# A mixture-of-experts decoder layer on one core: token rows of an expert pair picked by a 0/1 product from SBUF instead of gathered from memory

## The chip, the core and the metric

The kernel is one program on one NeuronCore of a Trainium2 chip. Its engines are PE (TensorE, matrix products), DVE (VectorE), ACT (ScalarE), POOL (GpSimd) and SP (SyncE, which here only issues transfers). The metric is the device time of one execution in microseconds, as the median of several runs: 1571.71 us for the kernel before (1568.71 to 1578.26 in 3 runs).

## The reference

One decoder layer in float32, width 2048, on 256 prompt tokens and 8 sample tokens, each of these with a cache of 2048 past positions in pages of 128. What matters here is the last part, the experts:

```python
lg = uf @ w_rg + b_rg                       # 4 groups, top-1
le = einsum('td,gde->tge', uf, w_re) + b_re # 8 experts in the group, top-2
comb = sum(one_hot(eid, 32) * gate[..., None], axis=1)
h = silu(einsum('td,edf->tef', u, w_gate)) * einsum('td,edf->tef', u, w_up)
h = h * comb[:, :, None]
return einsum('tef,efd->td', h, w_down)     # 32 experts, 2048 -> 256 -> 2048
```

The kernel computes each expert only for the tokens that chose it. Each of the 256 prompt tokens chooses two experts, so 512 rows of 2048 floats (8 KB) go to experts.

## The kernel before

**Stages.** The first part, `attention_and_route`, runs over 128 steps (`STEPS`), one page of a sample's cache in each. SP loads key and value pages into rings; DVE scores the keys, PE multiplies the values (`values`, L967). Between the pages the steps carry the prompt's projection, its attention heads, the output projection and, from step `ROUTE` = 111, the router. Step 122 (`PLACE`) has DVE build one-hot tables that say which token sits in which slot of which expert block; `slots` on PE (step 125) turns them into index lists by small matmuls.

**Token rows.** In steps 115 to 122 PE transposes the normalised tokens (`token_rows`, L1110), ACT copies them to the tile `qo` (L1336), 128 tokens at a time, and stores them as rows in the memory buffer `u_rows` (L1340). After the last page, POOL gathers by the index list `idx` the rows of the first two experts into `xg` (L952), a DMA with an index for each partition. PE turns them with 16 transposes (`first_tokens`, L1155) and ACT copies the result to `xgT` (L1346). Then come the sample tokens' own output projection (L1171) and sums, and a barrier.

**Expert pairs.** The second part, `experts`, works on two experts at a time, 16 pairs; each expert has 64 slots. For a pair SP loads six blocks of 2 MB (gate, up and down weights of two experts) into six slots of the tile `ws`, each as soon as PE has used the block that lay in it: `gu0`, `gu1` free gate and up, `y0`, `y1` free down. All go through one queue, in the order gate, up, gate, up, down, down. PE does for a pair n: gate and up of the first expert (L1931, L1933), of the second, then transposes of the first result (`turn_over`, L1940), the token rows of pair n+1 (`tokens`, 16 transposes, L1921), `turn_over` of the second, and the down products of both (L1953). Before these it waits until ACT has copied the next `xgT` (L2030). POOL gathers the rows of pair n+2 (L1853) once PE has transposed those of n+1, as there is one `xg`, and then scatters pair n's results to `y_rows` (L1867). A flag `many2` chooses between gathers of 64 and 128 indices; indices without a token are skipped. Up to five extra pairs for crowded experts stand behind flags, and none is used in these runs. In the first pair PE, DVE and ACT also do the sample tokens' routing (L1960, L1968, L2063), and ACT turns to the pair only after it.

At the end SP reads `y_rows` back, DVE adds and normalises, and the output is stored.

Of the kernel before, what the change touches and what calls it, by code (L numbers as in the profile page):

```python
# [50 lines left out]
C_SEMS = ("gsq gss gms gsqrt on od h sq2 ss2 ms2 sqrt2 un lp lpc lgp rt rcopy rst iota ex mask cnt pe2 oh idxp idx "  # L51
# [129 lines left out]
def hybrid_step(nc, a, outs, u_rows, y_rows):  # L181
    (y_prompt, y_sample, sbk_p, sbv_p, fxk_p, fxv_p, logf_p, sbk_s, sbv_s, fxk_s, fxv_s, logf_s) = outs
    ctx = ExitStack()
    with ctx:
# [28 lines left out]
        xg = sb("xg", [P, D])  # L213
        xgT = sb("xgT", [P, KC, P])
        idx = sb("idx", [P, PAIRS], I32)
# [4 lines left out]
        many2 = sb("many2", [1, PAIRS], I32)  # L220
# [72 lines left out]
        class start:  # L293
# [296 lines left out]
            def vector(dve):  # L590
# [90 lines left out]
                for i in range(PAGES, 2 * PAGES):  # L681
                    score_half(i)
                    if i == PAGES:
# [5 lines left out]
                            cTs, FB, ptr, ws, W, kring, vring, qb, Z, key_caches, value_caches, w_in, bank, S, C, E, wr, br, xg, xgT, idx, dest,  # L689
                            gates, extra, many, many2, iota, destc, drow, xs_pc, g_pc, sqs, srs, outs, u_rows, start, A,  # L690
# [5 lines left out]
        experts(nc, ctx, ws, W, a, ident, ones, iota, gcol, lastq, xT, xn, xgT, xg, wr, br, bank, sem, E, idx, dest, gates, extra,  # L696
                many, many2, destc, drow, sqs, srs, y_prompt, y_sample, u_rows, y_rows)
# [19 lines left out]
HALF = SLOTS // 2  # L717

# [63 lines left out]
def attention_and_route(nc, a, ident, ones, tri_ge, tri_lt, neg_sb, neg_fx, pick, lastq, seg, gcol, xT, xn, qo, lf, qpart,  # L782
                        cTs, FB, ptr, ws, W, kring, vring, qb, Z, key_caches, value_caches, w_in, bank, S, C, E, wr, br, xg, xgT, idx, dest,
                        gates, extra, many, many2, iota, destc, drow, xs_pc, g_pc, sqs, srs, outs, u_rows, start, A,
# [7 lines left out]
    with ctx:  # L792
# [21 lines left out]
        ohs = take(2, 2, P)  # L814
        ohb = take(2, 2, PAIRS)
        ohb2 = take(2, 2, BLOCKS)
# [3 lines left out]
        slot_of = take(P)  # L820
# [5 lines left out]
        tok, tokc = take(3), take(3)  # L826
# [4 lines left out]
        ohs2 = rstd.rearrange("p t s -> p (t s)").rearrange("p (t k s) -> p t k s", t=2, k=2)  # L831
# [78 lines left out]
        def _(pool):  # L910
# [14 lines left out]
            own.step(pool.tensor_scalar(tokc[:, :], tok[:, :], -1.0, float(T), ALU.mult, ALU.add))  # L925
            own.step(pool.memset(manyf[:, :], 1.0))
            own.step(pool.iota(io32[:, :].rearrange("p (h b s) -> p h b s", h=2, b=2), [[HALF, 2], [SLOTS, 2], [1, HALF]],
                               base=0, channel_multiplier=0))
            own.step(pool.tensor_copy(slot_of[:, :], io32[:, :]))
# [16 lines left out]
            pool.wait_ge(S["bcast"], NB)  # L946
            own.step(pool.memset(xg[:, :], 0.0))
            pool.wait_ge(C["idx"], 1)
            pool.wait_ge(C["rst"], 32)
            for n in range(2):  # L950
                wait_past(pool, E["xgp"], 4 * n)
                pool.indirect_dma_start(xg[:, :], None, u_rows[0:SEQ, :],  # L952
                                        bass.IndirectOffsetOnAxis(ap=idx[:, n:n + 1], axis=0),
                                        bounds_check=SEQ - 1, oob_is_err=False).then_inc(E["xg"], 16)

        @block.tensor
        def _(pe):
# [177 lines left out]
            def slots():  # L1135
                pe.wait_ge(C["oh"], 1)
                pe.wait_ge(S["done2"], 1)
                for i in range(4):
                    pe.matmul(bank[7][:, 0:PAIRS], ohs[:, i // 2, i % 2, :], ohb[:, i // 2, i % 2, :],
                              start=(i == 0), stop=(i == 3))  # L1140
                pe.wait_ge(C["oh"], 2)
                for i in range(4):
                    mm = pe.matmul(bank[7][:, PAIRS:PAIRS + BLOCKS], ohs2[:, i // 2, i % 2, :], ohb2[:, i // 2, i % 2, :],
                                   start=(i == 0), stop=(i == 3))
                mm.then_inc(C["idxp"], 1)

            def first_tokens():
                pe.wait_ge(E["xg"], 16)
# [1079 lines left out]
```

## Time and profile before

| | |
|---|---|
| median of 3 runs | 1571.71 us (1568.71 to 1578.26) |
| profiled execution | 1566.98 us, span 1565.2 us |
| mean granted TensorE clock | 0.903 |
| busy: PE / DVE / ACT / POOL | 81% / 43% / 15% / 4% |
| read from memory, written | 568.74 MB, 17.77 MB |
| queue 0 (POOL's indirect transfers) | 4432 packets, 9.05 MB, 1.8% |
| stages | steps with pages to about 948 us, experts from 999 us, last weights landed about 1516 us |

The span runs from the first to the last instruction of the profiled execution. A granted clock of 1.00 is 2.4 GHz and 0.50 is 1.2 GHz. The DMA share is the mean busy share of the core's 16 DMA engines. PE's matmuls in float32 appear as two records each, its transposes as one.

### The profile page before, as it was taken

What the parts mean: (1) busy time and instruction counts of PE and PEld (TensorE: products, weight loads), DVE (VectorE), ACT (ScalarE), POOL (GpSimd) and SP (SyncE); (2) the same over time, 40 slices, a digit from 0 to 9 for tenths busy, and PEclk for the clock granted to TensorE, in tenths of its full rate; (3) what the DMA queues carried; (4) which work ended last, traced back from release to release, by engine and by line L of the source; (5) the groups of instructions that cost most, each with busy time, mean ns of one, the idle gap of its engine ahead of it and who ended that gap; (6) DMA issues with size and microseconds to landing.
All of it is one profiled execution on the core that took longest, in us unless ns stands there. A gap on an engine that the chain in (4) does not pass through costs nothing. (4 is left out here: it accounts for less than half of the span.)

```text
span 1565.2 us, 24701 instructions
## 1 busy us (share of the span) xinstructions
PE 1274.4 (81%) x7862; PEld 806.4 (52%) x7863; DVE 672.5 (43%) x4782; ACT 229.8 (15%) x453; POOL 61.8 (4%) x107
## 2 busy tenths in 40 slices
PE   7999788889889798847999977788787778678783
PEld 5777455556556466424667533544444444344451
DVE  4536855757657576758664671121000001000004
ACT  2121002212122122111020111011000010100011
POOL 1000000000000000001000000001000000100000
PEclk9999999999899899867999996789899998888996
DMA  9767999999999999999999899989999999999974
GB/s 310 269 205 292 389 389 394 384 392 375 375 400 378 382 396 372 410 402 374 374 403 402 330 410 367 422 346 415 399 421 382 390 389 371 369 387 386 376 338 172
DMA packets 173996, 576.64 MB, mean 368 GB/s; under 512 B 18457, under 2 KB 78666, under 8 KB 160058
## 3 DMA queue, kind: packets, MB, share of 16 engines
q1 hardware_dynamic: 145616, 541.70, 89.6%
q10 hardware_dynamic: 23842, 24.68, 4.6%
q0 software_dynamic: 4432, 9.05, 1.8%
q8 instruction: 42, 0.69, 0.2%
q14 instruction: 64, 0.52, 0.1%
HBM read 568.74 MB, written 17.77 MB: 375 GB/s over the span
## 5 line engine op out<-in xcount | busy, mean ns | idle before, releaser
L128 DVE CUSTOM_DVE_ANT_0 ws<-ws,xgT 128x128 f32<-128x128 f32 x1792 | 388.1, 284 | 200.9 <-DMA ws<-in_cache_fox_k 173.0
L1931 PE MATMUL bank<-ws,xgT 128*64 128x256 f32 x1024 | 261.0, 420 | 103.7 <-DMA ws<-in_w_expert_up 99.4
L982 PE MATMUL bank<-xn,ws 128*128 128x264 f32 x1152 | 291.0, 408 | 7.9 <-DMA ws<-in_w_in 7.9
L982 PEld LDWEIGHTS bank<-xn,ws 128*128 128x128 f32 x1152 | 223.8, 200 | 109.3 <-issue 55.5
L1933 PE MATMUL bank<-ws,xgT 128*64 128x256 f32 x1024 | 261.1, 420 | 0.0
L1931 PEld LDWEIGHTS bank<-ws,xgT 128*64 128x64 f32 x1024 | 152.9, 152 | 209.4 <-DMA ws<-in_w_expert_up 110.2
L967 PE MATMUL bank<-ws,PR 128*32 128x512 f32 x1024 | 149.2, 663 | 80.5 <-DMA ws<-in_cache_fox_v 76.2
L2131 DVE COPY gu<-bank 128x256 f32<-128x256 f32 x32 | 13.6, 425 | 386.9 <-PE bank L1933 386.9
L1933 PEld LDWEIGHTS bank<-ws,xgT 128*64 128x64 f32 x1024 | 152.8, 152 | 0.0
L128 DVE DVE_READ_ACCUMULATOR2_ANT Z<- 128x1 f32 x1792 | 142.1, 79 | 0.0
L1953 PE MATMUL bank<-ws,hT 128*32 128x512 f32 x1024 | 116.1, 606 | 12.3 <-ACT xgT L2030 12.1
L1087 PE MATMUL bank<-qo,ws 128*128 128x256 f32 x512 | 118.5, 391 | 5.6 <-DVE qo L1532 4.6
L1087 PEld LDWEIGHTS bank<-qo,ws 128*128 128x128 f32 x512 | 98.8, 195 | 31.1 <-issue 14.8
L521 PE MATMUL bank<-xn,ws 128*128 128x264 f32 x384 | 86.8, 387 | 0.0
L967 PEld LDWEIGHTS bank<-ws,PR 128*32 128x32 f32 x1024 | 21.5, 112 | 121.2 <-DMA ws<-in_cache_fox_v 90.3
L521 PEld LDWEIGHTS bank<-xn,ws 128*128 128x128 f32 x384 | 72.6, 190 | 14.1 <-issue 2.0
L1953 PEld LDWEIGHTS bank<-ws,hT 128*32 128x32 f32 x1024 | 32.4, 112 | 84.5 <-issue 69.6
L605 DVE CUSTOM_DVE_ANT_0 ws<-ws,xgT 128x128 f32<-128x128 f32 x256 | 55.3, 286 | 39.2 <-DMA ws<-in_cache_sb_k 14.6
L2038 ACT ACTIVATE si<-bank 128x128 f32<-128x128 f32 x32 | 8.8, 276 | 323.0 <-PE bank L1940 323.0
L2142 DVE COPY ys<-bank 128x512 f32<-128x512 f32 x32 | 20.6, 686 | 56.7 <-PE bank L1953 56.7
L1256 ACT ACTIVATE blk<-bank 128x264 f32<-128x264 f32 (+1 forms) x40 | 16.4, 410 | 180.5 <-PE bank L982 122.3
L1867 POOL DMA_INDIRECT y_rows<-ys,dest x32 | 29.1, 910 | 161.5 <-DVE ys L2142 124.5
(439 smaller groups left out, 979.0 us busy)
## 6 DMA issues: line engine op xcount, KB each, us to landing
ws<-in_cache_sb_k SPq DMA_DIRECT2D x128, 512.0 KB, 8.3
ws<-in_cache_fox_k SPq DMA_DIRECT2D x128, 512.0 KB, 12.9
ws<-in_cache_sb_v SPq DMA_DIRECT2D x128, 512.0 KB, 8.9
ws<-in_cache_fox_v SPq DMA_DIRECT2D x128, 512.0 KB, 12.7
ws<-in_w_expert_gate SPq DMA_DIRECT2D x32, 2048.0 KB, 21.9
ws<-in_w_expert_up SPq DMA_DIRECT2D x32, 2048.0 KB, 26.4
ws<-in_w_expert_down SPq DMA_DIRECT2D x32, 2048.0 KB, 25.4
ws<-in_w_in SPq DMA_DIRECT2D x24, 2048.0 KB, 21.3
```

The lines of the kernel that those rows point to most:

```text
L128: ins = dve.tensor_tensor_reduce(k, k, qb[:, (g * H + h) * HD:(g * H + h + 1) * HD], 1.0, 0.0, ALU.mult, ALU.add, Z[:, n % 2, g, h, t:t + 1])
L521: mm = pe.matmul(bank[4 + k % 4][:, 0:T], chunk(n)[:, c, m * P:(m + 1) * P], xn[:, c, :], start=(c == 0), stop=(c == KC - 1))
L605: ins = dve.tensor_tensor_reduce(k, k, qb[:, (g * H + h) * HD:(g * H + h + 1) * HD], 1.0, 0.0, ALU.mult, ALU.add, Z[:, 0, g, h, t:t + 1])
L967: mm = pe.matmul(bank[0][r0:r0 + 32, :], PR[:, g, t, :], vring[:, u, g, half * 512:(half + 1) * 512], start=(t == 0), stop=(t == PAGES - 1))
L982: mm = pe.matmul(out[:, 0:T], w[:, c, m * P:(m + 1) * P], xn[:, c, :], start=(c == 0), stop=(c == KC - 1))
L1087: mm = pe.matmul(out, ws[:, 4 + r, k0:k0 + P], qo[:, 8 * r + c, 0:SEQ], start=(r == 0 and c == 0 and m % 2 == 0), stop=(r == 1 and c == 7) ...
L1256: nc.scalar.activation(out, src, ACT.Copy).then_inc(S[done], 1)
L1867: pool.indirect_dma_start(y_half, bass.IndirectOffsetOnAxis(ap=dest[0:rows, 2 * n + k:2 * n + k + 1], axis=0), ys[k][0:rows, :], None, bou ...
L1931: pe.matmul(bank[2 * k][0:SLOTS, 0:256], lhs, ws[:, wg, c * 256:(c + 1) * 256], start=(c == 0), stop=(c == KC - 1))
L1933: mm = pe.matmul(bank[2 * k][SLOTS:P, 0:256], lhs, ws[:, wu, c * 256:(c + 1) * 256], start=(c == 0), stop=(c == KC - 1))
L1953: mm = pe.matmul(bank[4 + 2 * k + dc][q * HALF:(q + 1) * HALF, :], hT[k][:, j, h0:h0 + HALF], ws[:, wd, d0:d0 + 512], start=(j == 0), stop ...
L2142: dve.tensor_copy(ys[0][:, i * 512:(i + 1) * 512], bank[4 + i][:, :]).then_inc(E["yc0"], 1)
```

## The change

The tokens stay in `qo`. ACT now writes them so that `token_cols(qo, t, c)` is a block of 128 tokens by 128 of the 2048 columns, side by side; the store to `u_rows` and the gathers are gone. DVE's tables are kept: `in_slot` (is this the token's slot within the pair) and `in_pair` (is this its pair), in the room of `xg`. For each pair POOL multiplies them and adds the two choices of a token: `pick_tok[:, i, t, :]`, 128 tokens by 128 slots of zeros and ones, in two buffers. PE multiplies: for each of 16 column blocks two matmuls of 128x128 (one for each half of the tokens), which add up to the block of `xgT` that the transposes gave. PE's loop over pairs is written out for two pairs a turn, because of the two buffers, and the extra pairs are written out without a loop. `slots` loses the matmuls for `idx`, DVE its steps for `idx` and `many2`; `place` on DVE additionally waits for the last broadcast of queries, which has used the same tile.

PE, end of the first part, before. The names are: `ws<-...PR` value pages, `blk` the tables, `osum` and `pick` the last sample's output.

```order
L967 MATMUL bank<-ws,PR 32x512 x12
L1139 MATMUL bank<-blk 128x21 x4
L1143 MATMUL bank<-blk 128x42 x4
L967 MATMUL bank<-ws,PR 32x512 x8
L1055 MATMUL bank<-pick,osum 128x4 x4
L1155 MATMUL bank<-ident,xg 128x2x2x32 x16
L1161 MATMUL bank<-sred,ones 128x16
L1171 MATMUL bank<-ws,qo 32x512 x64
```

The same place in the changed kernel:

```order
L964 MATMUL bank<-ws,PR 32x512 x12
L1136 MATMUL bank<-blk 128x42 x4
L964 MATMUL bank<-ws,PR 32x512 x8
L1052 MATMUL bank<-pick,osum 128x4 x4
L1148 MATMUL bank<-xg,qo 128x128 x32
L1155 MATMUL bank<-sred,ones 128x16
L1165 MATMUL bank<-ws,qo 32x512 x64
```

Four matmuls of `slots` are gone, and 32 matmuls stand where 16 transposes stood.

PE in the loop over pairs, from the last gate and up matmul to the down products, before (`gu` the gate and up results, `hT` the input of down):

```order
L1933 MATMUL bank<-ws,xgT 64x256
L1940 MATMUL bank<-ident,gu 128x128 x2
L1914 ISA
L79 REGISTER_ALU
L1921 MATMUL bank<-ident,xg 128x2x2x32 x16
L1940 MATMUL bank<-ident,gu 128x128 x2
L1997 REGISTER_ALU
L1953 MATMUL bank<-ws,hT 32x512 x32
```

And in the changed kernel:

```order
L1914 MATMUL bank<-ws,xgT 64x256
L1919 REGISTER_ALU
L1921 MATMUL bank<-ident,gu 128x128 x2
L79 REGISTER_ALU
L1901 MATMUL bank<-xg,qo 128x128 x32
L1921 MATMUL bank<-ident,gu 128x128 x2
L1978 REGISTER_ALU
L1934 MATMUL bank<-ws,hT 32x512 x32
```

The place is the same, the rows' operands come from `qo` and the table, and there are 32 matmuls for 16 transposes.

The diff, cut to its core:

```diff
+        in_slot = xg[:, 0:4 * P].rearrange("p (t k s) -> p t k s", t=2, k=2)
+        in_pair = xg[:, 512:512 + 4 * PAIRS].rearrange("p (t k n) -> p t k n", t=2, k=2)
+        pick_tmp = xg[:, 640:640 + 4 * P].rearrange("p (t k s) -> p t k s", t=2, k=2)
+        pick_tok = xg[:, 1152:1152 + 4 * P].rearrange("p (i t s) -> p i t s", i=2, t=2)
...
+def token_cols(qo, t, c):
+
+    return qo[:, 8 * t + c // 2, c % 2 * P:(c % 2 + 1) * P]
...
-            pool.wait_ge(S["bcast"], NB)
-            own.step(pool.memset(xg[:, :], 0.0))
-            pool.wait_ge(C["idx"], 1)
-            pool.wait_ge(C["rst"], 32)
+            pool.wait_ge(C["oh"], 1)
             for n in range(2):
-                wait_past(pool, E["xgp"], 4 * n)
-                pool.indirect_dma_start(xg[:, :], None, u_rows[0:SEQ, :],
-                                        bass.IndirectOffsetOnAxis(ap=idx[:, n:n + 1], axis=0),
-                                        bounds_check=SEQ - 1, oob_is_err=False).then_inc(E["xg"], 16)
+                own.step(pool.tensor_tensor(pick_tmp.rearrange("p t k s -> p (t k) s"), in_slot.rearrange("p t k s -> p (t k) s"),
+                                            over(in_pair[:, :, :, n].rearrange("p t k -> p (t k)"), P), ALU.mult))
+                pool.tensor_tensor(pick_tok[:, n, :, :], pick_tmp[:, :, 0, :], pick_tmp[:, :, 1, :], ALU.add).then_inc(E["xg"], 1)
+                pool.wait_ge(E["xg"], n + 1)
...
             def first_tokens():
-                pe.wait_ge(E["xg"], 16)
+                pe.wait_ge(E["xg"], 1)
...
                 for k in range(4):
                     for c in range(4):
-                        out = bank[4 + k][:, c * P:(c + 1) * P].rearrange("p (b h s) -> p h b s", b=2, h=2)
-                        mm = pe.transpose(out, xv[:, 4 * k + c, :], ident[:, :])
+                        for t in range(2):
+                            mm = pe.matmul(bank[4 + k][:, c * P:(c + 1) * P], token_cols(qo, t, 4 * k + c), pick_tok[:, 0, t, :],
+                                           start=(t == 0), stop=(t == 1))
                     mm.then_inc(E["xgp"], 1)
...
             def token_rows(i):
                 t, k = divmod(i, 4)
                 act.wait_ge(C["rt"], i + 1)
-                h0 = 8 * t + 2 * k
-                nc.scalar.activation(qo[:, h0:h0 + 2, 0:SEQ], bank[(4, 6)[i % 2]][:, :].rearrange("p (a f) -> p a f", a=2),
+                to = qo[:, 8 * t:8 * t + 8, 0:SEQ].rearrange("p a (b f) -> p a b f", b=2)[:, :, :, 32 * k:32 * k + 32]
+                nc.scalar.activation(to, bank[(4, 6)[i % 2]][:, :].rearrange("p (f a b) -> p a b f", a=8, b=2),
                                      ACT.Copy).then_inc(C["rcopy"], 1)
-                if k == 3:
-                    act.wait_ge(C["rcopy"], i + 1)
-                    act.dma_start(u_rows[t * P:(t + 1) * P, :].rearrange("p (a f) -> p a f", f=SEQ),
-                                  qo[:, 8 * t:8 * t + 8, 0:SEQ]).then_inc(C["rst"], 16)
...
             def tokens(n):
 
-                rest = pool.value_load(many2[0:1, n:n + 1], min_val=0, max_val=1)
-                wait_past(pool, E["xgp"], 4 * n)
-                with pool.If(rest > 0):
-                    gather(n, P)
-                with pool.Else():
-                    gather(n, SLOTS)
+                pool.tensor_tensor(pick_tmp.rearrange("p t k s -> p (t k) s"), in_slot.rearrange("p t k s -> p (t k) s"),
+                                   over(in_pair[:, :, :, n].rearrange("p t k -> p (t k)"), P), ALU.mult).then_inc(E["sel"], 1)
+                pool.wait_ge(E["sel"], n - 1)
+                wait_past(pool, E["xgp"], 4 * n - 4)
+                pool.tensor_tensor(pick_tok[:, n % 2, :, :], pick_tmp[:, :, 0, :], pick_tmp[:, :, 1, :], ALU.add).then_inc(E["xg"], 1)
+                pool.wait_ge(E["xg"], n + 1)
...
-            with pe.Fori(1, EXP_PAIRS - 1) as n:
-                pair(n, True)
+            with pe.Fori(0, EXP_PAIRS // 2 - 1) as m:
+                for i in range(2):
+                    pair(2 * m + 1 + i, True, i=i)
```

## Rows read from the trace of the kernel before

**Rows 1.** The page: DMA queues (packets, MB, share), chain of waits.

```profile
q10 hardware_dynamic: 23842, 24.68, 4.6%
q0 software_dynamic: 4432, 9.05, 1.8%
DMA ws<-in_w_expert_up 23%; PE bank L1931 8%; PE bank L1953 1%; DMA ws<-y_rows 1%; SPq L170 0%; PE bank L1933 0%; PE bank L1960 0%; DVE ws L2173 0%; DMA y_rows<-ys,dest 0%; DVE ws L2162 0%; DVE ws L2156 0%; ACT xgT L2030 0%; ACT L2038 0%; DVEq L1813 0%; PE bank L1968 0%
```

**Rows 2.** Windows: us, busy time by engine, granted clock, DMA share, GB/s.

```profile
915.00:948.00 33.00, 23.75 (x146) 10.03 (x138) 19.48 (x80) 3.68 (x7) 0.38 (x1) 0.79 1.04 408
1050.00:1500.00 450.00, 351.09 (x2862) 193.09 (x2862) 36.93 (x83) 46.98 (x110) 36.34 (x39) 0.90 0.99 391
964.00:969.00 5.00, 5.00 (x32) 1.28 (x28) 0.00 (x0) 0.00 (x0) 0.00 (x0) 0.58 0.62 199
1033.00:1038.00 5.00, 5.00 (x36) 1.29 (x32) 0.83 (x2) 0.00 (x0) 0.00 (x0) 0.65 0.15 31
```

**Rows 3.** Timeline of SP: start, us, what; second gate load of two pairs.

```profile
1149.28 0.33 SPq L170 DMA_DIRECT2D ws<-in_w_expert_gate  x1
...
1492.84 0.33 SPq L170 DMA_DIRECT2D ws<-in_w_expert_gate  x1
```

**Rows 4.** Timeline of one steady pair's turn, with the idle time before in brackets.

```profile
1252.98 0.51 PE L1940 MATMUL bank<-ident,gu 128*128 128x128 f32 x2
...
1253.32 1.97 PE L1921 MATMUL bank<-ident,xg 128*128 128x128 f32 x16
...
1255.93 7.07 PE L1953 MATMUL bank<-ws,hT 128*32 128x512 f32 x64 [0.40 <-ACT xgT L2030]
...
1269.07 0.69 PE L1931 MATMUL bank<-ws,xgT 128*64 128x256 f32 x1 [6.07 <-DMA ws<-in_w_expert_up]
...
1277.83 0.33 SPq L170 DMA_DIRECT2D ws<-in_w_expert_gate  x1
...
1279.79 0.43 PE L1931 MATMUL bank<-ws,xgT 128*64 128x256 f32 x1 [2.16 <-DMA ws<-in_w_expert_up]
```

**Rows 5.** Timeline of the end of the first part.

```profile
934.01 0.69 DVE L1600 TENSOR_TENSOR blk<-blk 128x512 f32<-128x512 f32 x1
...
939.25 1.93 PE L967 MATMUL bank<-ws,PR 128*32 128x512 f32 x8 [1.29 <-DMA ws<-in_cache_fox_v]
...
948.83 1.05 PE L1055 MATMUL bank<-pick,osum 128*128 128x4 f32 x8 [0.73 <-issue]
...
956.35 3.68 PE L1155 MATMUL bank<-ident,xg 128*128 128x128 f32 x16 [6.46 <-DMA xg<-u_rows,idx]
```

**Rows 6.** Timeline and groups of PE (busy, mean ns): float32 matmuls of 128x128.

```profile
44.28 1.05 PE L538 MATMUL bank<-zx,blk 128*128 128x128 f32 x8
...
L538 PE MATMUL bank<-zx,blk 128*128 128x128 f32 x16 | 2.1, 275 | 0.0
```

**Rows 7.** Windows of 1 us, columns as in rows 2.

```profile
948.00:949.00 1.00, 0.27 (x6) 0.17 (x2) 0.00 (x0) 0.60 (x1) 0.76 (x1) 1.00 1.05 391
1255.00:1256.00 1.00, 0.60 (x9) 0.41 (x11) 0.00 (x0) 1.00 (x3) 0.00 (x0) 1.00 0.80 295
1269.00:1270.00 1.00, 0.93 (x6) 0.55 (x8) 0.00 (x0) 0.00 (x0) 0.00 (x0) 0.50 1.11 463
```

**Rows 8.** Timeline of PE and of ACT in the first pair.

```profile
1030.49 10.03 PE L1953 MATMUL bank<-ws,hT 128*32 128x512 f32 x64 [6.59 <-ACT xgT L2030]
...
1028.59 1.85 ACT L2030 ACTIVATE xgT<-bank 128x448 f32<-128x448 f32 x4
```

**Rows 9.** Timeline of POOL: a cast, a steady pair's gather.

```profile
711.11 0.33 POOL L922 CAST iota<-io 128x128 f32<-128x128 int32 x1
...
1220.60 0.96 POOL L1853 DMA_INDIRECT xg<-u_rows,idx  x1 [24.80 <-PE bank L1921]
```

**Rows 10.** Windows of 6 us in two turns, columns as in rows 2.

```profile
1156.00:1162.00 6.00, 3.05 (x32) 0.65 (x20) 1.07 (x2) 1.08 (x2) 1.77 (x2) 1.00 1.01 423
1225.00:1231.00 6.00, 2.36 (x24) 0.52 (x16) 0.37 (x1) 1.09 (x2) 1.99 (x2) 1.00 1.02 262
```

More of the change, by code:

```diff
@@ L695, in hybrid_step @@
         bctx.close()
-        experts(nc, ctx, ws, W, a, ident, ones, iota, gcol, lastq, xT, xn, xgT, xg, wr, br, bank, sem, E, idx, dest, gates, extra,
-                many, many2, destc, drow, sqs, srs, y_prompt, y_sample, u_rows, y_rows)
+        experts(nc, ctx, ws, W, a, ident, ones, iota, gcol, lastq, xT, xn, qo, xgT, in_slot, in_pair, pick_tmp, pick_tok, wr, br, bank, sem, E, dest, gates, extra,
+                many, destc, drow, sqs, srs, y_prompt, y_sample, y_rows)
 STEPS = NB * PAGES
@@ L1760, in attention_and_route, with experts @@
         bstack.close()
-def experts(nc, ctx, ws, W, a, ident, ones, iota, gcol, lastq, xT, xn, xgT, xg, wr, br, bank, sem, E, idx, dest, gates, extra,
-            many, many2, destc, drow, sqs, srs, y_prompt, y_sample, u_rows, y_rows):
+def experts(nc, ctx, ws, W, a, ident, ones, iota, gcol, lastq, xT, xn, qo, xgT, in_slot, in_pair, pick_tmp, pick_tok, wr, br, bank, sem, E, dest, gates, extra,
+            many, destc, drow, sqs, srs, y_prompt, y_sample, y_rows):
     def sb(name, shape, dt=F32, where=ctx):
@@ L1910, in _, with tokens @@
         def _(pe):
-            def tokens(n, stored):
-                pe.wait_ge(E["xg"], 16 * n + 16)
+            def tokens(n, stored, i):
+                pe.wait_ge(E["xg"], n + 1)
                 wait_past(pe, E["yc0"], 2 * stored)
                 wait_past(pe, E["yc1"], 2 * stored)
-                xv = xg[:, :].rearrange("s (p c) -> s c p", c=KC)
                 for k in range(4):
                     for c in range(4):
-                        out = bank[4 + k][:, c * P:(c + 1) * P].rearrange("p (b h s) -> p h b s", b=2, h=2)
-                        mm = pe.transpose(out, xv[:, 4 * k + c, :], ident[:, :])
+                        for t in range(2):
+                            mm = pe.matmul(bank[4 + k][:, c * P:(c + 1) * P], token_cols(qo, t, 4 * k + c), pick_tok[:, i, t, :],
+                                           start=(t == 0), stop=(t == 1))
                     mm.then_inc(E["xgp"], 1)
@@ L1978, in sample_rest, with pair @@
                 pe.matmul(bank[4][:, P:P + 2], spread[:, :], gates[0:NB, 2, :], start=True, stop=True).then_inc(F["hs"], 1)
-            def pair(n, ahead, first=False, last=False):
+            def pair(n, ahead, first=False, last=False, i=0):
                 pe.wait_ge(E["xgT"], 4 * n + 4)
@@ L2001, in pair @@
                 down(1, n)
[L2003 to L2011 removed]
+            pair(0, True, True, i=1)
+            with pe.Fori(0, EXP_PAIRS // 2 - 1) as m:
+                for i in range(2):
+                    pair(2 * m + 1 + i, True, i=i)
+            pair(EXP_PAIRS - 1, False, last=True)
+            with pe.If(in_use(pe, 0) > 0):
+                for n in range(EXP_PAIRS, PAIRS):
+                    with pe.If(in_use(pe, 2 * (n - EXP_PAIRS)) > 0):
+                        tokens(n, n, n % 2)
+                        pair(n, False)
             for i in range(8):
```

64 lines of the change are left out of this document (19 added, 45 removed).

## The prediction

> **What bounds the kernel now.** I read the windows first, for the two stretches that the change touches: a DMA share of 1.04 at 408 GB/s in 915 to 948 us, and 0.99 at 391 GB/s in 1050 to 1500 us [rows 2]. The chain of waits agrees: its largest item by far is the load of the up weights, 23% [rows 1]. So bytes are the currency there. But the chain also has a part without DMA, and it matters: from about 948 to 1038 us the order is set by PE, ACT and DVE, and the transfers run dry twice, at 964 to 969 us (share 0.62) and at 1033 to 1038 us (0.15) [rows 2].
>
> In steady state a pair's turn is (1492.84 - 1149.28) / 10 = 34.36 us, from the issues of the second gate load [rows 3]. PE's part in it: first gate and up 1269.07 to 1277.83, 8.8 us; wait 2.2; second gate and up from 1279.79, 7.3; from turn-over to the end of down 1252.98 to 1263.00, 10.0; wait for weights 6.1. That makes 34.4 (7.3 is what the others leave), of which 8.3 are waits for DMA [rows 4].
>
> **The change part by part.** *The store of the token rows goes.* It is 256 rows of 8 KB, 2.10 MB. They flow while PE waits for value pages (1.29 us is shown for one) [rows 5]. At the 408 GB/s of that stretch they take 5.1 us. Upper end: queue 10 needs 4.6% of 1565 us for 24.68 MB, 2.9 us per MB, so 6.1 us [rows 1]; lower end 0, if something else took their place. I take 5.1, since the value pages wait for DMA right there. What is late next is the 0/1 table: it is done at 934.7 (end of L1600) [rows 5], and the pages before `slots` would end near 936, so it just keeps up. Half of the matmuls in `slots` go too; the waits for pages cover them, so I count 0; without that cover they would add to the gain.
>
> *The first gather goes, the first product comes.* PE is free at 949.88, waits 6.46 us for the gather, and ends its 16 transposes at 960.03: 10.15 us [rows 5]. The table is there 10 us before, so PE goes straight on. The product is 32 matmuls 128x128, each with new weights. The program's fp32 matmuls stand in the trace as two records, transposes as one: eight records of L538, 128x128 with changing weights, take 1.05 us, one alone 0.275: (1.05 - 0.275) / 7 = 0.111 us from start to start [rows 6]. 64 records: 63 x 0.111 + 0.275 = 7.27 us. Gain 2.9 us. The other end is the half clock at which the transposes ran, 3.68 against 1.97 us in the steady pairs [rows 4, 5], less one record's own time 0.217 us each: 14.1 us, a loss of 4.0. I take full speed: the clock is 1.00 at 948 to 949, the transposes ran slowly after a stop of 6.46 us, and the product follows L1055 at once [rows 5, 7].
>
> The Trainium skill ("TensorE: Matmul & The Clock Gate", Part 1) says that the throttled state is the default and that activity releases it, idleness brings it back. By that rule, too, the product starts at full speed if the last value pages have warmed the array, and at half if they haven't; the first case gives the gain, the second is a rival below.
>
> So expert work starts 5.1 + 2.9 = 8.0 us earlier. The transfers follow: the w_out loads that PE frees come 8 us sooner, and the queue ahead of them is shorter by the store and two gathers, 6.4 us, so the dry spot at 964 does not grow.
>
> *The first pair.* Its product (7.27 in place of 1.97 us) costs nothing: PE has 6.59 us idle after the transposes until ACT, late in that pair, has copied xgT at 1030.44 [rows 8]. The extra 5.3 us leave 1.3 of that cover; without it they would count one for one. It gives something back: PE no longer idles, so down should run at full clock, 7.07 instead of 10.03 us [rows 4, 8]. Gain 3.0, lower end 0. It lies on the path, because the transfers stand still until the down slots are free, 1033 to 1038 [rows 2].
>
> *The steady pairs.* Each gather moved its share of 256 tokens x 2 experts x 8 KB = 4.19 MB, 0.262 MB a pair. At 391 GB/s that is 0.67 us; by queue 0's own time (1.8% of 1565 us for 9.05 MB, 3.1 us per MB) 0.81 [rows 1]. I take 0.75, between the two. Thirteen gathers lie after 1038 us: 9.7 us (8.7 to 10.6). PE's turn grows by 7.27 - 1.97 = 5.3 us, 26.1 to 31.4, against a turn of 33.6: hidden in the 8.3 us of waits. With the wait of 6 us mostly filled, the cold start of the next gate and up (8.8 against 7.3 us) would go as well. Down frees its two slots 5.3 us later; their loads stand behind four gate and up loads, 8.4 MB or 21 us at 391 GB/s, so the queue does not run dry.
>
> *POOL.* It loses 16 gathers of about 1 us and gets two elementwise operations each, 128x512 and 128x256. The nearest row is its cast of 128x128, 0.33 us [rows 9]; in proportion 1.3 and 0.7 us, 2 together. POOL has waited 24.80 us before its gather [rows 9], so 0. If the cover were gone, the 2 us would count in each pair. The wait for the earlier product (E["xgp"]) stands ahead of `store`, but is met before down starts. The loop written out twice and ACT's strided copy are hidden in the same way.
>
> **Sum:** 5.1 + 2.9 + 3.0 + 9.7 = 20.7 us from the profiled execution's 1566.98 us: 1546. The median shown is 4.7 higher, which would give 1551. I say 1549. The forecast's own range is 1538 to 1556.
>
> **Rivals.**
> 1. *Cold first product.* The page steps before it don't fill PE, which waits for each page [rows 5]; if the clock is down, the first term turns from -2.9 to +4.0. Against: 1.00 at 948 [rows 7]. Total 13.8 us less: 1553 to 1558. Chance 0.12.
> 2. *The gathers were free.* If a turn isn't set by bytes but by the order of the six loads, only 11 us are left: 1556 to 1561. Against: share 0.99 over 450 us. Chance 0.12.
> 3. *The gathers cost more than their bytes.* In most turns the transfers fall to some 262 GB/s for 6 us, beginning 5 us after the gather's issue at 1220.60; undisturbed it is 423 [rows 9, 10]. If that goes with the gathers, (423 - 262) / 423 x 6 = 2.3 us more for each of 11 turns, 25 us: 1521 to 1526. Against: the turn at 1156 has gather and scatters and no dip, and the scatters, which stay, are in flight as well. The Trainium skill ("DMA: Bandwidth & Descriptors", Latency and other measured facts) guesses that descriptors written by GpSimd slow two of the DMA engines, which would speak for it; the same goes for the scatters. Chance 0.10.
> 4. *PE becomes the bound, slower than before.* Place: the product between the turn-overs. From 1.97 + 8.3 - 0.75 = 9.5 us per product PE sets the turn. At half clock it takes 14.1 us: turn 26.1 - 1.97 + 14.1 = 38.2, 13 x 3.9 = 50 us lost, and the start gains only 1: 1616 to 1621. For: the clock does fall in every turn, to 0.50 at 1269. Against: it falls in the wait for weights and is 1.00 at 1255, where the transposes run [rows 4, 7]. Chance 0.05.
> 5. *The change does not do what it says,* or its time is taken back by a transfer I don't see: within 1%. Chance 0.04.
>
> The forecast has 0.57. A measurement of this kernel tells about 1% (15.7 us) from no change. The forecast's own range reaches below that line, so I give 0.44 of its 0.57 to faster; with rival 3 that makes 0.54. Rivals 1, 2, 5 and the rest of the forecast: 0.41. Slower: 0.05. The range takes in rivals 1 and 2 with their spread and half the way to rival 3: 1532 to 1564.
>
> **What would show it.** In the profile after: no u_rows and no xg transfers, queue 0 near 4.9 MB; 64 records of the product in 7.3 us, in the first one at a granted clock near 1; the first gate and up matmul some 8 us earlier; down of the first pair in 7 us; a turn of 33.6 us; PE waits for weights of about 3 us a turn. I am wrong if the turn stays at 34.4 (rival 2), falls to 31 to 32 (rival 3), or if PE never waits for the up weights (rival 4).

## The result and the profile after

The changed kernel takes 1517.77 us (median of 4 runs, 1516.05 to 1519.66), the kernel before 1570.21 (4 runs, 1567.69 to 1578.26): ratio 0.966, 95% interval 0.962 to 0.970. That is 52 us less. The forecast was 1549 with a range from 1532 to 1564, so the result lies below the range. The profiled execution took 1516.05 us.

The page of the kernel after, the rows that answer to [rows 1]; q0 is POOL's indirect transfers, q10 ACT's:

```profile
q10 hardware_dynamic: 21762, 22.58, 4.3%
q0 software_dynamic: 2896, 4.86, 0.9%
PE 17%; DMA 14%; DVE 1%; ACT 1%; issue 1%; SPq 0%; DVEq 0%; POOLq 0%; ACTq 0%; POOL 0%
```

The 2.10 MB of the store and the 4.19 MB of the gathers are gone, and PE now has a larger part of the chain that sets the end than DMA has.

Its windows (columns as in [rows 2]), then two second gate loads on SP, ten pairs apart, as in [rows 3]:

```profile
915.00:948.00 33.00, 24.31 (x156) 9.58 (x149) 23.02 (x83) 5.35 (x11) 4.15 (x4) 0.84 1.00 387
1050.00:1450.00 400.00, 383.41 (x3426) 249.04 (x3424) 35.29 (x78) 49.39 (x107) 45.52 (x50) 1.00 1.01 423
964.00:969.00 5.00, 5.00 (x52) 1.73 (x44) 0.00 (x0) 0.60 (x1) 0.00 (x0) 1.00 1.04 386
1027.00:1031.00 4.00, 4.00 (x42) 1.18 (x38) 1.05 (x2) 0.00 (x0) 0.00 (x0) 1.00 0.40 131
```

```profile
1135.23 0.33 SPq L170 DMA_DIRECT2D ws<-in_w_expert_gate  x1
...
1442.60 0.33 SPq L170 DMA_DIRECT2D ws<-in_w_expert_gate  x1
```

A turn is (1442.60 - 1135.23) / 10 = 30.74 us, where it was 34.36 and I had forecast 33.6. The transfers run at 423 GB/s at a DMA share of 1.01; before it was 391 at 0.99 [rows 2]. So the DMA engines were about as busy before and moved 8% less. The gathers' own bytes do not explain it: 0.262 MB in a turn is 2% of 12.8 MB.

Where the time went can be counted in the profiled executions, from the token counts' last matmul (L1127 before, L1124 after). The work ahead of it is nearly as it was, and its start differs from kernel to kernel (922 to 927 us in the profiles here). The kernel before:

```profile
922.15 0.63 PE L1127 MATMUL bank<-blk,ones 128*128 128x32 f32 x4
...
962.89 13.13 PE L1171 MATMUL bank<-ws,qo 128*32 128x512 f32 x96 [2.63 <-DVE qo L1643]
```

The kernel after (start, us, what, idle time before it; L1148 is the first product, L1165 the w_out product, L1934 the first pair's down):

```profile
924.68 0.63 PE L1124 MATMUL bank<-blk,ones 128*128 128x32 f32 x4
...
947.77 1.05 PE L1052 MATMUL bank<-pick,osum 128*128 128x4 f32 x8 [0.73 <-ACT osum L1250]
948.68 7.39 PE L1148 MATMUL bank<-xg,qo 128*128 128x128 f32 x64
...
958.94 10.51 PE L1165 MATMUL bank<-ws,qo 128*32 128x512 f32 x96 [2.73 <-DVE qo L1629]
...
1017.45 7.31 PE L1901 MATMUL bank<-xg,qo 128*128 128x128 f32 x64
1026.24 7.07 PE L1934 MATMUL bank<-ws,hT 128*32 128x512 f32 x64 [1.25 <-ACT xgT L2012]
```

| stretch, us | before | after | gain | forecast |
|---|---|---|---|---|
| counts to the start of the last sample's output product (L1055, L1052) | 26.7 | 23.1 | 3.6 | 5.1 |
| from its end to the w_out product's start | 13.0 | 10.1 | 2.9 | 2.9 |
| from there to the end of the first pair's down | 77.6 | 74.4 | 3.3 | 3.0 |
| in all, to the end of the first pair's down | 118.4 | 108.6 | 9.7 | 11.0 |

Ends are start plus duration: down of the first pair ends at 1040.52 before [rows 8] and at 1033.31 now. The 1.05 us of L1055 and L1052 are in the last line alone. From the end of that down product to the end of the span it is 524.7 us before and 481.0 now: 43.7 us less, where the forecast had 9.7 for the steady pairs. With the 9.7 above, less the 2.5 us by which the counts come later now (924.68 against 922.15), that is the 51 us between the two profiled executions.

### The profile page after: what moved, and what is told of

Read it like the earlier page. It is cut to its first block and busy times, and to the rows that moved or that the text cites. A ratio compares the mean times of both kernels' runs of the same rounds, so it can differ in the third digit from the quotient of the medians.

```text
span 1514.3 us, 26133 instructions
## 1 busy us (share of the span) xinstructions
PE 1315.7 (87%) x8622; PEld 870.3 (57%) x8622; DVE 673.4 (44%) x4778; ACT 233.6 (15%) x453; POOL 75.4 (5%) x119
## 3 DMA queue, kind: packets, MB, share of 16 engines
q0 software_dynamic: 2896, 4.86, 0.9%
## 5 line engine op out<-in xcount | busy, mean ns | idle before, releaser
L1912 PE MATMUL bank<-ws,xgT 128*64 128x256 f32 x1024 | 231.4, 386 | 16.7 <-DMA ws<-in_w_expert_up 12.1
L1914 PE MATMUL bank<-ws,xgT 128*64 128x256 f32 x1024 | 231.5, 386 | 0.0
L1912 PEld LDWEIGHTS bank<-ws,xgT 128*64 128x64 f32 x1024 | 140.3, 139 | 104.6 <-issue 22.2
L1914 PEld LDWEIGHTS bank<-ws,xgT 128*64 128x64 f32 x1024 | 140.3, 139 | 0.0
L1934 PE MATMUL bank<-ws,hT 128*32 128x512 f32 x1024 | 113.2, 594 | 7.1 <-ACT xgT L2012 6.9
L1901 PE MATMUL bank<-xg,qo 128*128 128x128 f32 x960 | 109.7, 275 | 0.0
L1901 PEld LDWEIGHTS bank<-xg,qo 128*128 128x128 f32 x960 | 108.5, 192 | 0.0
L1934 PEld LDWEIGHTS bank<-ws,hT 128*32 128x32 f32 x1024 | 32.0, 110 | 76.7 <-issue 67.0
L2120 DVE TENSOR_TENSOR hT<-si,bank 128x128 f32<-128x128 f32 x32 | 9.2, 288 | 108.3 <-ACT si L2020 108.2
## 6 DMA issues: line engine op xcount, KB each, us to landing
ws<-in_cache_fox_v SPq DMA_DIRECT2D x128, 512.0 KB, 12.8
```

What stands on the lines that cost most here:

```text
L1901: mm = pe.matmul(bank[4 + k][:, c * P:(c + 1) * P], token_cols(qo, t, 4 * k + c), pick_tok[:, i, t, :], start=(t == 0), stop=(t == 1))
L1912: pe.matmul(bank[2 * k][0:SLOTS, 0:256], lhs, ws[:, wg, c * 256:(c + 1) * 256], start=(c == 0), stop=(c == KC - 1))
L1914: mm = pe.matmul(bank[2 * k][SLOTS:P, 0:256], lhs, ws[:, wu, c * 256:(c + 1) * 256], start=(c == 0), stop=(c == KC - 1))
L1934: mm = pe.matmul(bank[4 + 2 * k + dc][q * HALF:(q + 1) * HALF, :], hT[k][:, j, h0:h0 + HALF], ws[:, wd, d0:d0 + 512], start=(j == 0), stop ...
```

## The experiments

In most turns of the kernel before, the transfers fall to some 262 GB/s for 6 us though the DMA engines are busy [rows 10]; I call this a slow stretch. Two theories stood first. **G**: the gathers disturb the weight stream far beyond their bytes (my third rival). **D**: the slow stretches come from when PE frees the weight slots, which its longer and warmer turn changes. Labels with b start from the kernel before, with a from the changed one. Steady window means 1050 to 1450 us. All diffs are cut to the lines that matter; those of experiments 5, 6, 9 and 10 are against the kernel of experiment 4. Ratios are to the kernel before as run again beside each group (medians 1569.55 to 1572.01 us); differences to the changed kernel are from its 1517.77.

**1. The kernel before without the steady gathers.**

```diff
-                with pool.If(rest > 0):
-                    gather(n, P)
-                with pool.Else():
-                    gather(n, SLOTS)
+                pool.memset(pad[:, 5:6], 0.0).then_inc(E["ng"], 1)
```

> The kernel before, without the 14 row gathers of pairs 3 to 16 (their tokens are computed from the rows of the second pair, so those experts' outputs are left wrong in value, not in amount of work); the store and the first two gathers stay, and PE's work is unchanged. **Theory G** (a gather costs the weight stream far more than its 0.26 MB: the 6 us stretches at about 260 GB/s in the trace before belong to it): the stretches go, the turn of the steady pairs falls from 34.4 to about 31 us, the time to 1525 to 1535. **Theory D** (the stretches come from when weight slots come free, which PE's shorter and colder turn sets): the turn falls by the bytes alone, 0.75 us, and the time is 1558 to 1563.

PE waits for this counter where it waited for the gather. 1531.11 us, ratio to before 0.974 (0.970 to 0.978). With PE's short turn of before, without a product, the stream runs at full rate. The gathers alone carry 38 of the 52 us. Theory D fails.

**2. The kernel before with a longer PE turn.**

```diff
+                    for again in range(4):
                         for c in range(4):
```

> The kernel before with its gathers, and with each pair's 16 transposes of token rows made four times over (64 PE records in place of 16, about 5.4 us more of PE work a pair, near to what the changed kernel's product takes). **Theory G**: the stretches at 260 GB/s stay, the turn stays at about 34 us and the time at 1565 to 1575 (PE has 8.3 us of waits a turn to take it). **Theory D**: with PE's longer turn, at full clock, the stretches go, the turn falls to about 31 us, and the time is 1520 to 1535.

1572.40 us, ratio 1.0015 (0.9995 to 1.0036). 5.4 us more of PE in each pair cost nothing and gain nothing that the runs can tell: the cover that the prediction named is there, and PE's turn is not the cause. In the first pair the longer work leaves PE idle for 1.17 us instead of 6.59, and down then takes 7.07 us, not 10.03 [rows 8]:

```profile
1038.70 7.07 PE L1954 MATMUL bank<-ws,hT 128*32 128x512 f32 x64 [1.17 <-ACT xgT L2031]
```

These 3 us do not show in the total; no run says what takes them back.

**3. The changed kernel with half of each steady product.**

```diff
-                        for t in range(2):
-                            mm = pe.matmul(..., token_cols(qo, t, 4 * k + c), pick_tok[:, i, t, :],
-                                           start=(t == 0), stop=(t == 1))
+                        mm = pe.matmul(..., token_cols(qo, 0, 4 * k + c), pick_tok[:, i, 0, :],
+                                       start=True, stop=True)
```

> The changed kernel with half of each steady pair's product (the first 128 tokens alone, so the rows of the others are left out of the experts' input; 32 PE records instead of 64, 3.6 us less of PE a pair). **Theory G**: no stretches at 260 GB/s, and with PE no longer the bound in the first turns the turn is at the transfers' pace, 30.4 to 30.7 us; time 1512 to 1522. **Theory D**: PE's turn is near that of the kernel before again, the stretches come back, the turn is 33 us or more, and the time 1540 to 1555.

1521.57 us, ratio 0.969 (0.966 to 0.972): the slow stretches do not return with a shorter PE turn, and the shorter product gains nothing. So the half that was left out costs nothing in the changed kernel. For the other half there is only experiment 2, where more PE work than the product adds was free beside the slower stream. In the first pair down is slow again after a longer idle time:

```profile
1023.40 9.44 PE L1933 MATMUL bank<-ws,hT 128*32 128x512 f32 x64 [4.84 <-ACT xgT L2011]
```

**4. The changed kernel plus a gather that nothing reads.**

```diff
+    pool.indirect_dma_start(xg2[0:SLOTS, :], None, a["x_prompt"][0],
+                            bass.IndirectOffsetOnAxis(ap=gi[0:SLOTS, 0:1], axis=0),
+                            bounds_check=SEQ - 1, oob_is_err=False).then_inc(E["gx"], 16)
```

> The changed kernel with one gather more a steady pair, of 64 indices of which half are in bounds (32 rows of 8 KB from the prompt's input, 0.26 MB, to a buffer that nothing reads), issued where the kernel before issued its own. Nothing else of the work changes. **Theory G**: the stretches at 260 GB/s are back, the turn rises to about 34 us, the time to 1555 to 1570. **Theory D**: the bytes alone, 0.6 us a turn where the transfers set it: 1520 to 1528.

1571.22 us, ratio to before 1.0005 (0.998 to 1.003). One unread gather a pair takes back all 52 us, 53.5 / 14 = 3.8 us each (the total is 1.2 us above the range of theory G). Theory G holds from both sides. The steady windows of the kernels so far, in the order of the experiments:

```profile
1050.00:1450.00 400.00, 334.90 (x2812) 186.43 (x2810) 35.72 (x79) 44.62 (x104) 25.55 (x40) 0.94 1.00 424
```

```profile
1050.00:1450.00 400.00, 359.55 (x3080) 229.18 (x3079) 32.58 (x72) 43.40 (x94) 32.15 (x35) 0.95 0.98 388
```

```profile
1050.00:1450.00 400.00, 352.43 (x2978) 206.20 (x2979) 35.29 (x78) 49.28 (x107) 45.40 (x50) 0.94 1.00 422
```

```profile
1050.00:1450.00 400.00, 351.22 (x2999) 219.89 (x2998) 31.86 (x70) 42.58 (x92) 55.54 (x60) 0.94 0.98 381
```

The last number decides: 424 and 422 GB/s without gathers, 388 and 381 with them, while PE's busy time (334.90 to 359.55 us) does not order them.

What in a gather costs 3.8 us? Next come its parts.

**5. The same gather with no row in bounds.** All 64 indices point past the end:

```diff
-            for lo, k in ((0, 1000.0), (8, -1000.0), (24, 1000.0), (40, -1000.0), (56, 1000.0)):
+            for lo, k in ((0, 1000.0),):
```

> The changed kernel with the extra gather of a steady pair as in a2_plus_gather (1571.22 us with it, 1517.77 without: 3.8 us a gather), but with all its 64 indices out of bounds, so that it moves no row. **Theory L** (what a gather costs the weight stream is in the launch: its descriptors, made by GpSimd, and their passage through the DMA engines, whether or not rows move): most of the 53 us stays, 1550 us or more. **Theory R** (it is the moved rows, 32 packets' worth of 8 KB rows from memory to one partition each): nearly all of it goes, 1515 to 1525 us.

1518.21 us, ratio 0.966 (0.963 to 0.968): nothing. Queue 0 has the launches but not the bytes: 4016 packets as in experiment 4, 4.86 MB as in the changed kernel.

```profile
q0 software_dynamic: 4016, 4.86, 1.0%
```

So it isn't the launch. The Trainium skill (DMA: Bandwidth & Descriptors, Latency and other measured facts) has a guess that the prediction weighed, that descriptors written by GpSimd slow some DMA engines; this run gives it no support, as 64 more of them a pair cost nothing.

**6. 32 indices, all in bounds,** to partitions 0 to 31 instead of 8 to 23 and 40 to 55:

```diff
-    pool.indirect_dma_start(xg2[0:SLOTS, :], None, ...  ap=gi[0:SLOTS, 0:1]
+    pool.indirect_dma_start(xg2[0:32, :], None, ...  ap=gi[0:32, 0:1]
```

> The changed kernel with the extra gather, but of 32 indices, all in bounds: the same 0.26 MB in 32 rows of 8 KB, to partitions 0 to 31. **Theory R**: the cost is that of the gather with half its indices out of bounds, 1560 to 1575 us. **Theory O** (it is the mix, indices that are skipped between others, or the spread over partitions): it falls by half or more, under 1545 us.

1547.90 us, ratio 0.986 (0.983 to 0.988): 30.1 us over the changed kernel, 2.15 a gather. Neither expectation: as many rows and bytes cost a bit over half. Besides their places, the addresses that they come from and the 32 unused indices differ; by experiment 5 such indices cost nothing by themselves.

**7. An ordinary transfer on ACT's queue, 32 rows to 32 partitions.**

```diff
+                    act.dma_start(xg2[0:32, :], a["x_prompt"][0, 0:32]).then_inc(E["gx"], 16)
```

> The changed kernel with an ordinary transfer a pair in place of the extra gather: 32 rows of 8 KB, 0.26 MB, from the same input to 32 partitions of a buffer that nothing reads, started on ACT's queue where ACT has copied the next pair's columns, with no indices. **Theory R**: whoever starts them, rows of 8 KB into one partition each disturb the stream: 1555 us or more. **Theory I** (it belongs to gathers by index on POOL's queue): the bytes alone, 0.6 us a pair where the transfers set the turn: 1518 to 1530 us.

1544.68 us, ratio 0.984 (0.981 to 0.987): 26.9 / 15 = 1.8 us each. My bound for "rows disturb" was 1555; nearly what experiment 6 costs with indices, this costs without. Indices and POOL's queue have little part in it.

**8. The store put back.**

```diff
+                if k == 3:
+                    act.wait_ge(C["rcopy"], i + 1)
+                    act.dma_start(u_rows[t * P:(t + 1) * P, :]..., qo[:, 8 * t:8 * t + 8, 0:SEQ]).then_inc(C["rst"], 16)
```

> The changed kernel with the store of the token rows (2.10 MB to memory, two transfers on ACT's queue) put back in the first part; nothing reads it. My prediction gave the store 5.1 us of the sum. **Theory B** (its bytes stand in line with the value pages, as the prediction had it): 1522 to 1524 us, and the last score product of the first part ends some 5 us later. **Theory S** (it fell where the stream had room, since the rate in the changed kernel at 927 to 934 us is down to 229 to 311 GB/s without it): 1517 to 1520 us, at most 1.5 us later there.

1523.11 us, ratio 0.969 (0.967 to 0.972), 5.3 us over the changed kernel (the two intervals overlap, so the size is uncertain by some us). The kernel with the store, the rows from before:

```profile
925.13 0.63 PE L1124 MATMUL bank<-blk,ones 128*128 128x32 f32 x4
...
950.82 1.87 PE L1052 MATMUL bank<-pick,osum 128*128 128x4 f32 x8 [0.72 <-ACT osum L1250]
952.55 9.59 PE L1148 MATMUL bank<-xg,qo 128*128 128x128 f32 x64
...
965.00 10.51 PE L1165 MATMUL bank<-ws,qo 128*32 128x512 f32 x96 [2.73 <-DVE qo L1634]
```

From the counts to L1052 it is 25.7 us, against 23.1 without: 2.6 us, half of the 5.1. That fits a slack spot of the stream there (334 GB/s in 927 to 934 us of the changed kernel), which some of the store can fill. The first product takes 9.59 us instead of 7.39, at a granted clock of 0.50 until 956 us. But this needs no store. Nine kernels here have the changed kernel's first part without it: the changed one and experiments 3 to 7 and 9 to 11. The same product takes 7.39 us in four of their profiles and 8.72 to 10.29 in five. Experiment 5, for one, at a granted clock of 0.50 in 950 to 956 us:

```profile
951.65 10.13 PE L1148 MATMUL bank<-xg,qo 128*128 128x128 f32 x64
```

So the time agrees with B, and the path with something between B and S.

Now two theories of the rows, which go to SBUF, the on-chip memory of 128 partitions. **P**: it matters onto how few of the ways into SBUF they fall. **E**: it matters how many rows one DMA engine gets.

**9. The extra gather spread over 128 partitions.**

```diff
-    pool.indirect_dma_start(xg2[0:SLOTS, :], None, ...  ap=gi[0:SLOTS, 0:1]
+    pool.indirect_dma_start(xg2[:, :], None, ...  ap=gi[:, 0:1]      # index in bounds in every fourth partition
```

> The changed kernel with the extra gather of 32 rows of 8 KB (0.26 MB) a pair, but its rows go to every fourth of 128 partitions (128 indices, three of four out of bounds). So far: rows to partitions 8 to 23 and 40 to 55 cost 53 us over the kernel without (3.8 us a gather), to 0 to 31 they cost 30 us (2.1). **Theory P** (what counts is onto how few paths into SBUF the rows fall, beside weight transfers that want all of them): spread over all 128 partitions they cost little more than their bytes: 1522 to 1532 us. **Theory E** (what counts is how many rows fall to one DMA engine, four in the first of these, two in the second, two here): as in a4_all_in, 1543 to 1552 us. The Trainium skill, page SBUF — State Buffer, section Door 1: The DMA port swizzle, gives partitions 0 to 63 eight of sixteen ports and puts partitions 32 apart on one port; by it these rows reach 4 ports in a2_plus_gather, 8 in a4_all_in and 16 here.

1526.77 us, ratio 0.969 (0.965 to 0.973): 9.0 / 14 = 0.64 us a gather, what 0.262 MB take at 423 GB/s (0.62). These are the 32 rows of experiment 6 from the same addresses, with even more indices; the places differ, and 2.15 us have become 0.64. Theory E expected no change.

**10. Two gathers of 16 rows,** to partitions 0 to 15 and 32 to 47.

```diff
+                    for j in range(2):
+                        pool.indirect_dma_start(xg2[32 * j:32 * j + 16, :], None, ...  ap=gi[0:16, 0:1]
```

> The changed kernel with two gathers a pair of 16 rows of 8 KB each (together the same 0.26 MB), all indices in bounds, the first to partitions 0 to 15, the second to 32 to 47. Launches by themselves cost nothing (a3_none_in). **Theory P** (how few paths into SBUF; by the cited page partitions 32 apart share one): these rows are packed as closely as in a2_plus_gather, and cost as much: 1562 to 1575 us. **Theory E** (rows to one DMA engine: one of each gather, two in all, as in a4_all_in): 1543 to 1552 us.

1558.89 us, ratio 0.990 (0.987 to 0.993): 41 / 14 = 2.9 us a pair. This is 3 us under the range of P and 7 over that of E. Clearly dearer than 32 rows in partitions 0 to 31 (2.15), cheaper than experiment 4 (3.8). So half of the rows moved 32 partitions away cost more than all side by side, as P has it, but the crowding does not tell the whole cost.

**11. The transfer of experiment 7 over 128 partitions.**

```diff
-                    act.dma_start(xg2[0:32, :], a["x_prompt"][0, 0:32])
+                    act.dma_start(xg2[:, :], a["x_prompt"][0, 0:32].rearrange("r (c d) -> (r c) d", c=4))
```

> The changed kernel with the ordinary transfer of a5_act_direct (15 a kernel, 0.26 MB each, 1544.68 us), from the same addresses, but laid out over all 128 partitions, 2 KB in each, in place of 8 KB in each of 32. **Theory P**: the bytes alone, 0.6 us a pair: 1520 to 1530 us. **Theory B** (a second queue's transfer of that size disturbs the stream wherever it lands): as in a5_act_direct, 1540 to 1548 us.

1528.03 us, ratio 0.972 (0.968 to 0.975): 10.3 / 15 = 0.7 us each, the bytes, in place of 1.8. Its packets are smaller too (2 KB in place of 8), but in experiment 9 they were not.

**12. The kernel before, its rows spread.** The order of the slots changes, and the transposes undo it; every gather has 128 indices:

```diff
-   pool.iota(io32[...].rearrange("p (h b s) -> p h b s", h=2, b=2), [[HALF, 2], [SLOTS, 2], [1, HALF]], ...
+   pool.iota(io32[...].rearrange("p (b s h) -> p b s h", h=2, b=2), [[SLOTS, 2], [1, HALF], [HALF, 2]], ...
-   out = bank[4 + k][:, c * P:(c + 1) * P].rearrange("p (b h s) -> p h b s", b=2, h=2)
+   out = bank[4 + k][:, c * P:(c + 1) * P].rearrange("p (b h s) -> p b s h", b=2, h=2)
-                with pool.If(rest > 0): ...
+                gather(n, P)
```

> The kernel before, whole and with its gathers, with another order of the slots alone: a token of slot s of the pair's expert b is gathered to partition 64b + 2s, not 32b + s, so that the 32 or so rows of a pair lie on every second partition from 0 to 30 and from 64 to 94, and the transposes put their columns back in the same places (the gathers have 128 indices, the unused ones out of bounds). **Theory P**: most of what the gathers cost beyond their bytes goes: 1530 to 1545 us, a turn of 31 to 32 us. **Theory E**: rows are still four to some engines or two to all, at best as in a4_all_in: 1550 to 1570 us.

The experts' token slots begin at 8, so most rows lie on every second partition from 16 and from 80 up, not from 0 and 64 as the expectation says; the spread is the same. 1538.39 us, ratio 0.978 (0.975 to 0.981): 33.6 us faster than before with every gather in place. It is 7.3 us above the kernel without steady gathers (experiment 1), and 14 gathers at 423 GB/s take 8.7. What they cost beyond their bytes is gone. A spread gather's PE side costs nothing either: 16 transposes take 1.97 us as in [rows 4].

```profile
1205.35 1.97 PE L1917 MATMUL bank<-ident,xg 128*128 128x128 f32 x16
```

**The same stretch in four kernels.** Windows that begin 3 to 4 us after the extra or own gather's issue, with the clock, the DMA share and GB/s as the last numbers: experiment 4 (8 to 23 and 40 to 55), experiment 6 (0 to 31), experiment 9 (every fourth), and the kernel before with spread rows. The kernel before has 262 GB/s in such a stretch [rows 10].

```profile
1224.00:1230.00 6.00, 6.00 (x58) 2.54 (x52) 1.29 (x2) 1.08 (x2) 1.23 (x2) 1.00 0.95 257
```

```profile
1222.00:1227.00 5.00, 5.00 (x50) 2.06 (x44) 1.23 (x2) 1.08 (x2) 1.00 (x1) 1.00 0.99 279
```

```profile
1214.00:1220.00 6.00, 6.00 (x60) 2.73 (x54) 1.16 (x2) 1.09 (x2) 1.70 (x2) 1.00 1.00 417
```

```profile
1212.00:1218.00 6.00, 3.02 (x32) 0.65 (x20) 1.04 (x2) 1.08 (x2) 1.79 (x2) 1.00 1.01 423
```

The DMA engines are busy in all four, but in the first two they move 61 to 66% as much. The trace's list of packets says what they are busy with (packets that start in 1050 to 1450 us; a weight packet has 16 KB, a gathered row 8 KB):

```
kernel                        8 KB rows, median ns   16 KB weight packets, mean ns   turn longer than by bytes
before                                418                       655                       yes
experiment 4 (8-23, 40-55)            461                       666                       yes
experiment 6 (0-31)                   476                       639                       yes, less
experiment 9 (every fourth)           313                       621                       no
experiment 12 (every second)          309                       621                       no
after                                   -                       621                        -
```

Undisturbed, 8 KB take 309 ns and 16 KB 612 ns (medians), 26.5 and 26.8 GB/s for one engine. In the slow stretch of the kernel before, all 66 weight packets that start between 1225 and 1230 us take 798 to 1287 ns. So the crowded rows hold up their own packets and every weight packet beside them. By their size each weight packet should fill one partition (2 MB in 128 of 16 KB), and most of these partitions are far from the rows; what passes the delay on to them no trace shows.

**A test that the kernel before holds already.** It has two turns in which many rows move and the stream stays whole. They are the ones whose gather has the form for crowded experts, 128 indices; it takes POOL 1.02 to 1.03 us, the form with 64 indices 0.96 to 0.97:

```profile
1086.00 1.03 POOL L1853 DMA_INDIRECT xg<-u_rows,idx  x1 [18.50 <-PE bank L1921]
...
1152.22 1.02 POOL L1853 DMA_INDIRECT xg<-u_rows,idx  x1 [22.90 <-PE bank L1921]
```

They move 62 and 63 rows, twice the usual number. From slot 32 on an expert's rows go to partitions 64 and up, and the slots below, 8 to 31 of two experts, hold 48 at most, so at least 14 and 15 rows lie there. The rows take 309 to 316 ns, and the weight packets beside them 611 to 628. So twice the bytes, more widely placed, make no slow stretch, and it is the places again, in the kernel's own gathers.

The Trainium skill (SBUF — State Buffer, Door 1: The DMA port swizzle) states a rule that fits: SBUF takes transfers through 16 ports, partitions 0 to 63 reach 8 of them, and partitions 32 apart share one. By it the extra rows fall on 4 ports in experiment 4 and 10, on 8 in experiments 6 and 7, on 16 in 9, and on up to 16 in 12, and a weight load of 128 partitions wants all. The costs come in this order: 3.8 and 2.9, then 2.15 and 1.8, then 0.64 and 0.5 us. The traces show no ports, and that all weight packets are slow is more than this rule says.

## Why the prediction was wrong

**The step that failed** is "The steady pairs": "At 391 GB/s that is 0.67 us; by queue 0's own time ... 0.81. I take 0.75". It priced a gather by its bytes, and by the time of its own packets. What a gather takes from others is in neither. Thirteen gathers were to give 9.7 us. Taking the 14 steady ones out gave 38 (experiment 1), 2.7 us each; putting one a pair back cost 53.5 (experiment 4). With the rows spread the same gathers cost 0.5 us each (7.3 / 14), and from that kernel to the changed one it is 1538.39 - 1517.77 = 20.6 us. My sum for the whole change was 20.7. So the sum was that of a kernel whose gathers cost their bytes; this kernel's did not. That the two agree within 0.1 us is in part chance: the steady gathers count 7.3 in it where I had 9.7, and all the rest 1531.11 - 1517.77 = 13.3 where I had 11.0.

**The rate, too, was read in the wrong direction.** I took 391 GB/s as the stream's pace and divided by it. It was a mean of 423 and of the slow stretches, and the gathers made those.

**Rival 3 was the right one, at 0.10.** I had the dip of 262 GB/s and its start 5 us after the gather's issue, and held two things against it: the turn at 1156 without a dip, and the scatters in flight. The scatters are innocent (experiments 1 and 5 keep them at 424 and 422 GB/s); they bring rows of 4 KB out of SBUF, not in. The turn at 1156 was no evidence against it: its gather has 63 rows in the wide form, as shown above, and I took it for one like the others. The rival's price, 2.3 us a turn for 11 turns on top of the bytes, gave 1521 to 1526, and 1517.77 is 3 to 8 us below. Most turns before have a second, shallower dip (356 GB/s at a share of 0.93 in 1208 to 1212 us); some remain in the changed kernel (344 at 0.95 in 1424 to 1428 us), and how much of the difference they carry is not shown.

**The store, 5.1:** experiment 8 costs 5.3, but that is in part luck. What the term stood for, value pages that come later, is 2.6 us in experiment 8 and 3.6 between before and after. In the nine profiles with the changed first part the stretch from the counts to L1052 takes 21.4 to 24.2 us (median 23.1), in the four that start from the kernel before 25.5 to 26.7: some 3 us. Another 2.2 of the 5.3 can be the first product's clock, which falls without the store too. So the term was oversized, the error small beside the gathers'.

**First gather and first product, 2.9:** 13.0 against 10.1 us from L1055 or L1052 to the w_out product. The 64 records took 7.39 us, foretold 7.27, at full clock. That it ran at full clock here was luck: rival 1, a cold product, came in part in five of the nine profiles with this first part (8.72 to 10.29 us), and in experiment 8 (9.59). I had given it 0.12. Its price is 1.3 to 2.9 us there, not the 6.9 of a product that is cold to its end.

**The first pair's down at full clock, 3.0:** 7.07 us, where it was 10.03 [rows 8]. Right, and for the reason given: down takes 7.07 as well in experiment 2 after 1.17 us of idle time, and 9.44 in experiment 3 after 4.84. The extra 5.3 us of product are hidden as foretold. The transfers still run low once (0.40 at 1027 to 1031), but 6 us sooner.

**Expert work 8 us earlier:** 6.7, from the counts (77.0 us to its first matmul before, 70.3 after).

**PE's turn hidden, POOL at 0:** experiments 2 and 3 show it for PE, as far as each goes. The forecast expected 3 us of waits for weights a turn and a PE turn of 31.4; in the first four turns of the loop there is no such wait and PE sets the turn at 29.25 us, under the 30.7 that the transfers set later, and from 1200 to 1450 us the waits are 9.3 us, about 1.2 a turn. Rival 4 (half clock) did not come: 1.00 over the whole steady window. POOL's two operations take 1.06 to 1.18 and 0.73 to 1.06 us.

**What stays open.** How crowded rows slow all weight packets is not shown. Nor is it why 2.9 us in experiment 10 and 3.8 in experiment 4, with rows as crowded by the cited rule: experiment 4 has one burst of 32 rows where experiment 10 has two of 16, and perhaps more rows for some DMA engines (the traces do not say which engine carries which row). None of the runs separates these. That taking the real gathers out gave less (38) than adding the made one cost (53) has one cause in the two wide gathers, which disturb nothing, and in one of 11 rows alone; whether that is all of it is open.

## What to carry to other kernels

A transfer's price beside a saturated stream need not be bytes over rate: ask how many partitions its destination has and which ones. Where the DMA share stays near 1.0 while GB/s drops to 60%, the packets themselves have become slow; here the cause had been issued some 4 us earlier. A turn that does not fit the pattern deserves the question what differs in it: here it was a gather over more partitions, the later cure. Before a gather is removed, try its rows spread over all 128 partitions: here the order of slots gave 33.6 of the 52 us.

## What the hardware showed besides

- Indices out of bounds cost nothing that the runs can tell in this setting: with 64 of them a pair, 14 times, it is 1518.21 us against 1517.77.
- One of DVE's operations took twice as long beside POOL's. The kernel after:

```profile
935.59 1.06 POOL L948 TENSOR_TENSOR xg<-xg 128x512 f32<-128x512 f32 x1 [214.10 <-DVE xg L1583]
935.78 1.42 DVE L1587 TENSOR_TENSOR blk<-blk 128x512 f32<-128x512 f32 x1
```

The same operation (L1600 before) took 0.69 us [rows 5]. The Trainium skill (SBUF — State Buffer, Who interferes with whom) has a VectorE operation with two SBUF inputs and a GpSimd operation that reads SBUF exclude each other by a lock on a shared port; these rows agree, and GpSimd's started first. What it cost the kernel, if anything, no run shows.
